# Combining three attention groups: pairs of token tiles share their small steps, and ScalarE makes the third product

## The reference, cut to what matters

```python
wts = jax.nn.softmax(jnp.stack(lses), axis=0)
attn = jnp.einsum('gbsh,gbshd->bshd', wts, jnp.stack(outs)).reshape(b, s, ATTN_WIDTH).astype(x.dtype)
attn_branch = jnp.einsum('bse,ed->bsd', attn * jax.nn.silu(gate_a), w_br_a)
```

## Time and profile before

| | |
|---|---|
| median of 3 runs | 2629.17 us |
| profiled execution, its own time | 2635.06 us |
| its span | 2633.3 us |
| TensorE matmul busy | 2522.2 us, 96% |
| VectorE busy | 1616.7 us, 61% |
| ScalarE busy | 938.1 us, 36% |
| GpSimd busy | 478.6 us, 18% |
| mean granted TensorE clock | 0.984 |

### The profile page before, as it was taken

The page is one execution under the profiler, slowest core; times in us unless marked ns, Lnnn a source line. Parts: engine busy times, 40 slices in busy tenths (PEclk is TensorE's granted clock), DMA queues, the critical chain, the costliest instruction groups (busy, mean ns, idle before and its releaser), DMA issues. The chain is left out here.

```text
span 2633.3 us, 36120 instructions
## 1 busy us (share of the span) xinstructions
PE 2522.2 (96%) x14232; PEld 1541.7 (59%) x14232; DVE 1616.7 (61%) x2315; ACT 938.1 (36%) x1823; POOL 478.6 (18%) x462
## 2 busy tenths in 40 slices
PE   7999998999999999999799999999879999999997
PEld 4444343356666767676688888655434444444586
DVE  5747656636565656565679999767873235533543
ACT  5322222235555555555643433322531113211232
POOL 0105554400000000010035354332100000000000
PEclk9999999999999999999899999999889999999999
DMA  5824545423333424243753434445431120110132
GB/s 195 303 96 157 204 152 176 180 96 109 127 131 117 145 102 169 104 166 120 255 207 117 176 129 146 159 160 188 157 106 60 34 80 29 36 33 32 57 97 80
DMA packets 145263, 341.26 MB, mean 130 GB/s; under 512 B 8137, under 2 KB 102581, under 8 KB 138056
## 3 DMA queue, kind: packets, MB, share of 16 engines
q1 hardware_dynamic: 126312, 238.94, 26.6%
q0 software_dynamic: 18640, 93.72, 9.3%
q10 hardware_dynamic: 144, 6.29, 0.7%
HBM read 215.10 MB, written 130.12 MB: 131 GB/s over the span
## 5 line engine op out<-in xcount | busy, mean ns | idle before, releaser
L1288 PE MATMUL ps<-mem 128*128 128x512 f16 (+1 forms) x9312 | 1750.2, 348 | 24.0 <-ACT mem L1671 5.8
L1288 PEld LDWEIGHTS ps<-mem 128*128 128x128 f16 x9312 | 928.1, 102 | 815.4 <-issue 83.2
L847 ACT ACTIVATE mem<-mem 128x2048 f16<-128x2048 f32 (+1 forms) x56 | 108.6, 1940 | 390.3 <-DVE mem L865 390.2
L2155 DVE TENSOR_TENSOR mem<-ps,mem 128x512 f32<-128x512 f32 (+2 forms) x144 | 79.8, 554 | 235.1 <-PE ps L1421 234.4
L872 DVE SCALAR_TENSOR_TENSOR mem<-mem 128x2048 f16<-128x2048 f32 (+1 forms) x56 | 132.7, 2369 | 80.1 <-ACT mem L847 80.1
L1772 ACT ACTIVATE mem<-ps 128x512 f32<-128x512 f32 (+1 forms) x144 | 72.1, 500 | 307.6 <-PE ps L1434 307.2
L835 POOL PARTITION_ALL_REDUCE mem<-mem x56 | 45.1, 807 | 750.9 <-DVE mem L828 725.1
L1540 PE MATMUL ps<-mem 128*128 128x256 f32 x768 | 171.4, 380 | 0.6
L1475 PE MATMUL ps<-mem 128*128 128x256 f32 (+1 forms) x640 | 168.7, 422 | 0.0
L1540 PEld LDWEIGHTS ps<-mem 128*128 128x128 f32 x768 | 144.5, 190 | 24.2 <-issue 5.5
L2190 DVE TENSOR_TENSOR mem<-mem 128x1024 f16<-128x1024 f32 x96 | 117.1, 1220 | 48.3 <-ACT mem L1793 47.8
(11 more groups left out here) (190 smaller groups left out, 2604.0 us busy)
## 6 DMA issues: line engine op xcount, KB each, us to landing
s_ks<-mem SPq DMA_DIRECT2D x96, 512.0 KB, 2.7
mem<-s_ks SPq DMA_DIRECT2D x23, 2048.0 KB, 9.0
mem<-in_w_in SPq DMA_DIRECT2D x44, 1024.0 KB, 6.3
s_sums<-mem POOLq DMA_DIRECT2D x24, 1024.0 KB, 4.3
mem<-s_sums SPq DMA_DIRECT2D x48, 512.0 KB, 3.9
s_uc<-mem POOLq DMA_DIRECT2D x24, 768.5 KB, 6.1
mem<-s_uc SPq DMA_DIRECT2D x18, 1024.0 KB, 7.3
s_og<-mem POOLq DMA_DIRECT2D x72, 132.0 KB, 2.6
```

Source lines behind the costliest of these rows:

```text
L847: act.activation(w_place(b)[:, 0, 0:chunks(b)], raw_of(b), ACT.Copy, scale=wscale[b % 3]).then_inc(S["w_hi"], 1)
L1288: mm = pe.matmul(out, lhs(a, k), rhs(b, k), start=(k == 0 and x == 0), stop=(k == kc - 1 and x == 2))
L2155: dve.tensor_tensor(l[:, :, c0:c1], ps[:, 2 + N % 2, :].rearrange("p (x c) -> p x c", x=2)[:, :, c0:c1], bias, ALU.add).then_inc(S["a_bias ...
```

## The change

- The tiles are taken in pairs. The minima, differences and weights of tiles t and t + 1 are computed together at the even tile, with 12 instructions on VectorE (before, 8 for each tile) and one exponential on ScalarE for both. The differences and the last products, which have one instruction before, have three, one for each group, with no wait between them.
- The wait for the loaded data is then for both tiles of the pair.
- The third group's product leaves VectorE. A new function `weigh(t)` on ScalarE makes it by eight Copy instructions of 128x64, each scaled by one head's weight, into `third[t % 2]`. VectorE waits for it (`g_third`) before its last sum.
- `weigh(0)` stands on ScalarE right behind `combine(0)` and `weigh(1)` before the sixth gate tile's evacuation; `weigh(x + 2)` stands where the list has `T` x. `combine` stands only where x is even.
- The buffers `ogt` and `cmb` have four tiles in place of two. GpSimd loads tiles 0 to 3 before the last store of `s_hy`, and tile t when tile t - 4 is combined. The places of `w_allmax` and `b_allmax` behind tiles 4, 6, 7 and 10 stay.

```diff
             def load_og(t):
-                pool.dma_start(ogt[t % 2], og_d[:, P * t:P * t + P, :, :].rearrange("g p a c -> p g a c")).then_inc(ld_og[t % 2], 16)
+                pool.dma_start(ogt[:, t % 4], og_d[:, P * t:P * t + P, :, :].rearrange("g p a c -> p g a c")).then_inc(ld_og[t // 2 % 2], 16)
...
-                        load_og(0)
-                        load_og(1)
+                        for t in range(4):
+                            load_og(t)
...
-            for t in range(2, NT):
-                pool.wait_ge(S["g_cmb"], t - 1)
+            for t in range(4, NT):
+                pool.wait_ge(S["g_cmb"], t - 3)
                 load_og(t)
                 if t in (4, 7):
                     w_allmax(pool, M0 + 3 + (t - 4) // 3)
...
-            def combine(t):
-                act.wait_ge(S["g_sc"], 2 * t + 1)
-                act.activation(wts[t % 2][:, 8:32], wts[t % 2][:, 8:32], ACT.Exp).then_inc(S["g_exp"], 1)
+            def combine(k):
+                act.wait_ge(S["g_sc"], 2 * k + 1)
+                act.activation(wts[k % 2][:, 16:64], wts[k % 2][:, 16:64], ACT.Exp).then_inc(S["g_exp"], 1)
+
+            def weigh(t):
+                act.wait_ge(S["g_sc"], 2 * (t // 2) + 2)
+                if t >= 2:
+                    act.wait_ge(S["g_cmb"], t - 1)
+                e = wts[t // 2 % 2][:, 16 + 24 * (t % 2) + 16:16 + 24 * (t % 2) + 24]
+                for j in range(2 * HH):
+                    op = act.activation(third[t % 2][:, HD * j:HD * j + HD], ogt[:, t % 4, 2, j // HH, HD * (j % HH):HD * (j % HH) + HD], ACT.Copy,
+                                        scale=e[:, j:j + 1])
+                op.then_inc(S["g_third"], 1)
...
-                if n in (3, 5):
-                    combine(n // 2 - 1)
+                if n == 3:
+                    combine(0)
+                    weigh(0)
+                if n == 5:
+                    weigh(1)
...
+                    if x % 2 == 0 and x + 2 < NT:
+                        combine(x // 2 + 1)
                     if x + 2 < NT:
-                        combine(x + 2)
+                        weigh(x + 2)
...
+                if t % 2 == 0:
...
+                    dve.wait_ge(ld_og[t // 2 % 2], 32 * (t // 4 + 1))
...
+                    for g in range(3):
+                        op = dve.tensor_tensor(both[:, :, g], low, nm[:, :, g], ALU.subtract)
...
+                    for g in range(3):
+                        op = dve.tensor_tensor(both[:, :, g], both[:, :, g], total, ALU.mult)
...
-                if t >= 2:
-                    m_wait(dve, POS["T", t - 2, 0])
+                if t >= 4:
+                    m_wait(dve, POS["T", t - 4, 0])
...
                 chain(dve.tensor_tensor(acc, acc, tmp, ALU.add))
                 settle()
-                weighted(tmp, 2)
-                settle()
-                dve.tensor_tensor(acc, acc, tmp, ALU.add).then_inc(S["g_cmb"], 1)
+                dve.wait_ge(S["g_third"], t + 1)
+                dve.tensor_tensor(acc, acc, third[t % 2], ALU.add).then_inc(S["g_cmb"], 1)
```

More of the change, by code:

```diff
@@ L431, in build @@
         gated = hg_tile(KD * len(SPANS) - 1)
[L432 to L435, removed]
+        ogt = mem[:, MERGED:MERGED + 4 * 6 * OW].rearrange("p (t g a c) -> p t g a c", t=4, g=3, a=2)
+        GSC = MERGED + 4 * 6 * OW
+        wts = [mem[:, GSC + 128 * i:GSC + 128 * i + 128] for i in range(2)]
+        cmb = [mem[:, GSC + 256 + 2 * AW * i:GSC + 256 + 2 * AW * (i + 1)].rearrange("p (a c) -> p a c", a=2) for i in range(4)]
+        third = [mem[:, GSC + 256 + 8 * AW + AW * i:GSC + 256 + 8 * AW + AW * (i + 1)] for i in range(2)]
+        assert GSC + 256 + 10 * AW <= OUT
         m16 = halves(mem[:, BASE:BASE + KD * T], KD, T)
@@ L453, in build @@
             p_first p_hi p_lo f_r f_im f_y f_post
-            ld_hx ld_ftab ld_itab g_cmb g_sc g_exp m_mul b_maxed b_alled b_scaled b_hi b_lo h_hi h_lo m_acc o_sq o_root o_r o_y""".split()
+            ld_hx ld_ftab ld_itab g_cmb g_third g_sc g_exp m_mul b_maxed b_alled b_scaled b_hi b_lo h_hi h_lo m_acc o_sq o_root o_r o_y""".split()
         S = {n: sem(n) for n in names}
@@ L1607, in _ @@
                 for j in range(4):
-                    mm = pe.transpose(ps[:, n % 8, P * j:P * j + P], cmb[x % 2][:, 0, P * j:P * j + P], ident)
+                    mm = pe.transpose(ps[:, n % 8, P * j:P * j + P], cmb[x % 4][:, 0, P * j:P * j + P], ident)
                 mm.then_inc(bank_ready[n % 8], 1)
@@ L2429, in _ @@
             for t in range(NT):
[L2430 to L2437, removed]
@@ L2438, in _ @@
-                settle()
[L2439 to L2452, removed]
-                if t >= 2:
-                    m_wait(dve, POS["T", t - 2, 0])
+                o, w = ogt[:, t % 4], wts[t // 2 % 2]
+                acc, tmp = cmb[t % 4][:, 0, :], cmb[t % 4][:, 1, :]
+                both = w[:, 16:64].rearrange("p (t g a h) -> p t g a h", t=2, g=3, a=2)
@@ new lines, in _ @@
+                e = both[:, t % 2]
+                if t % 2 == 0:
+                    two = ogt[:, t % 4:t % 4 + 2]
+                    nm, den = two[:, :, :, :, HW:HW + HH], two[:, :, :, :, HW + HH:OW]
+                    low, total = (w[:, c:c + 16].rearrange("p (t a h) -> p t a h", t=2, a=2) for c in (0, 112))
+                    ed = w[:, 64:112].rearrange("p (t g a h) -> p t g a h", t=2, g=3, a=2)
+                    dve.wait_ge(ld_og[t // 2 % 2], 32 * (t // 4 + 1))
+                    chain(dve.tensor_tensor(low, nm[:, :, 0], nm[:, :, 1], ALU.min))
+                    settle()
+                    chain(dve.tensor_tensor(low, low, nm[:, :, 2], ALU.min))
+                    settle()
+                    for g in range(3):
+                        op = dve.tensor_tensor(both[:, :, g], low, nm[:, :, g], ALU.subtract)
+                        if g < 2:
+                            chain(op)
+                    op.then_inc(S["g_sc"], 1)
+                    dve.wait_ge(S["g_exp"], t // 2 + 1)
+                    chain(dve.tensor_tensor(ed.rearrange("p t g a h -> p (t g) a h"), both.rearrange("p t g a h -> p (t g) a h"),
+                                            den.rearrange("p t g a h -> p (t g) a h"), ALU.mult))
+                    settle()
+                    chain(dve.tensor_tensor(total, ed[:, :, 0], ed[:, :, 1], ALU.add))
+                    settle()
+                    chain(dve.tensor_tensor(total, total, ed[:, :, 2], ALU.add))
+                    settle()
+                    chain(dve.reciprocal(total, total))
+                    settle()
+                    for g in range(3):
+                        op = dve.tensor_tensor(both[:, :, g], both[:, :, g], total, ALU.mult)
+                        if g < 2:
+                            chain(op)
+                    op.then_inc(S["g_sc"], 1)
+                    settle()
+                    dve.wait_ge(S["g_sc"], t + 2)
```

## The result

The changed kernel takes 2627.09 us, the median of 20 runs (2614.98 to 2631.49). The kernel before, run beside it, takes 2639.03 us in 20 runs (2629.15 to 2646.84). The ratio is 0.9949, 95% interval 0.9937 to 0.996, so the change makes it 0.5% faster: of 2639 us some 13.5 (10.6 to 16.6). The two medians differ by 11.9. The forecast was 11.4 less. The forecast time of 2617.8 us, with its range of 2612.5 to 2623.0, was missed, because it was built on the three runs of before that were shown (2629.17), and these are the three fastest of the 20.

A forecast was written before the change was run, and what follows sets the result against it. VectorE was taken to bound the combining stage's end; its terms summed to -11.25 us, a tile-by-tile walk gave 11.6 less, and -11.4 was taken from 2629.17 us: 2617.8 us, range 2612.5 to 2623.

The forecast's parts named there:

- start of tile 2: VectorE starts tile 2 at 1860.5 us instead of 1861.27, -0.8 us.
- five even rounds: VectorE's even rounds: small steps +0.54, third product -0.73, wait for copies +0.11; -0.08 us each, -0.4 in all.
- five odd rounds: VectorE's odd rounds lose small steps (1.94 us) and the third product (0.73); -2.67 us each, -13.35 in all.
- load 5 at the pair (4, 5): Load 5, queued on GpSimd behind `w_allmax`, lands late for the pair; +3.8 us, bounds 1.9 and 4.4.
- tile 10: VectorE's wait for the exponential at tile 10 begins 0.2 us later through longer steps; -0.2 us.
- wait for T 11: The last gate product's wait for TensorE's transposes, 0.67 us before, gets shorter; -0.3 us.
- ScalarE's copies: Third product on ScalarE: 346 ns a copy, eight in 2.1 us, 2.2 with handshakes; even tiles wait 0.1 us.
- the prediction's w: ScalarE-bound rival, chance 0.07: eight copies take w us, even tiles stall w - 2.0; even at 3.4, 9.8 us slower at 4.5.
- Tile 1: VectorE waits some 2 us for `third`, but the next gate product can't start before transposes and evacuation end anyway.
- The wait for load 11: Load 11 stands behind `b_allmax(1)`, but VectorE waits for ScalarE's `span_hi(1)` and exponential until about its landing.
- The tail: What follows the last gate product, up to TensorE's long run from 1969 us, is untouched, so its gain passes through.
- The drain behind a table load: Rival: each ScalarE table switch also empties the engine for another 1.28 us; gain only 2.9 us, 2626.3 us, chance 0.03.

The follow-up runs named there:

- the loads first: Changed kernel with GpSimd's maxima behind the loads of tiles 5, 7, 9, 11 instead of 4, 6, 7, 10; ratio to before 0.9927.
- the low half later: The loads first, tile 10's exponential before ScalarE's high half, third weight block's low half and next maximum behind tile 3, `weigh(3)` earlier; ratio to before 0.9922.
- eight copies' worth of 3 and 4 us: Changed kernel with four or eight extra unread ScalarE copies ahead of each tile's eight; stretches 116.25 and 123.02 us, ratios to before 0.9975 and 0.9995.

## Why the prediction was right, and where it was wrong

**The step that failed** is the last of the sum: "the median of the runs is 5.9 us lower, and I take the difference over unchanged: 2629.17 - 11.4 = 2617.8 us". The 11.4 us was near, the 2629.17 was not this kernel's usual time. Of 20 runs of before three are those I had; the median of all is 9.9 us above them, and the range was drawn round the three as if they were exact. They lie within 0.7 us of each other, where the 20 spread over 17.7. The first three runs of the changed kernel also lie within 0.7 us (2628.35 to 2629.01), so that by these threes alone the change would be worth 0.6 us. Three runs that agree don't show how far a kernel spreads. 2629.17 x 0.9949 would be 2615.8, inside the range. The profiled execution's own 2635.06 us, 5.9 off the three, was the hint that the kernel varies by more than three runs show, and I treated it as an offset of the profile. The change was mis-sized too, by less: 11.4 us against the stretch's 13.4, most of it a table load in the tail that the sum put at nothing (below).

The variation lies ahead of the stage. Over the twelve profiled executions the mark in front of tile 0 comes between 1837.1 and 1858.0 us, while what follows the stretch takes 662.7 to 665.6. Two places carry most of it. TensorE's last product of L1372 (L1374 after) starts at 497.3 us before, 498.6 in the changed kernel's first profile, 507.2 with the loads first and 491.3 with the low half later. In the changed kernel's first profile another 6.5 us of its 7.9 arise between there and the first matmuls of L1558, 1321.0 before and 1328.8 after; in the other eleven profiles this part takes 820.9 to 825.6 us, in that one 830.2. Two waits of ScalarE for stores to `s_ks` are longer there, and then the same 18 matmuls take TensorE almost twice as long, before and then after:

```profile
1293.14 1.06 ACT L1793 ACTIVATE mem<-mem 128x1024 f16<-128x1024 f32 x1 [3.66 <-DMA s_ks<-mem]
...
1304.34 1.06 ACT L1793 ACTIVATE mem<-mem 128x1024 f16<-128x1024 f32 x1 [1.16 <-DMA s_ks<-mem]
...
1307.16 2.13 PE L1288 MATMUL ps<-mem 128*128 128x256 f16 x18
```

```profile
1295.23 1.06 ACT L1795 ACTIVATE mem<-mem 128x1024 f16<-128x1024 f32 x1 [4.42 <-DMA s_ks<-mem]
...
1308.18 1.06 ACT L1795 ACTIVATE mem<-mem 128x1024 f16<-128x1024 f32 x1 [3.09 <-DMA s_ks<-mem]
...
1311.56 4.05 PE L1290 MATMUL ps<-mem 128*128 128x256 f16 x18
```

The clock granted over these 18 matmuls is 1.00 before and 0.50 after; TensorE had idled 0.84 us shortly before them in the one and 2.77 us in the other. The instructions there are the same in both kernels. Why the stores landed later in one execution than in the other stays open; no experiment was made on it.

**Point by point**, predicted and measured, from the mark to the last gate product:

| term | predicted | measured |
|---|---|---|
| start of tile 2 | -0.8 | -0.62 |
| five even rounds | -0.4 | -1.02 |
| five odd rounds | -13.35 | -13.44 |
| load 5 at the pair (4, 5) | +3.8 | +3.06 |
| tile 10 | -0.2 | -0.18 |
| wait for T 11 | -0.3 | -0.26 |
| ScalarE's high half at tile 5 | 0 | +0.36 |
| sum | -11.25 | -12.10 |
| the sigmoid's table load in the tail | 0 | -1.28 |
| whole stretch | -11.25 | -13.38 |

- *What bounds the stage.* Right: adding and taking work on VectorE moved the end in each experiment until TensorE's transposes came up.
- *ScalarE's copies.* Right in kind, 0.1 us too dear: 333 ns each in place of 346, eight in 2.02 us. This is just under VectorE's 2.05 us of two products and a sum, so no even tile waits. With eight copies' worth of 3 and 4 us (the prediction's w) even tiles wait 1.0 and 1.95 us, about the w - 2.0 of the prediction, and the stretch gets 6.5 and 13.3 us longer, so the cover ends at once behind 2.05 us. That the walk came out even at w = 3.4 was 0.6 us too early: at 4.0 it is even.
- *Tile 1.* Right: VectorE waits 1.85 us for `third`, but the gate product behind it waits for ScalarE's evacuation anyway (0.53 us).
- *The loads.* Right in cause and place, by the experiment; load 5 landed 5.5 us after its issue and not 6.6. The wait for load 11 (1.88 us) was foreseen as covered by ScalarE's high half, and was.
- *The tail.* Wrong: "untouched" it is on VectorE, but the change ends ScalarE's loop with a Sigmoid, where it ended with an Exp, and so takes a table load out of the chain that follows. That is 1.3 us that no term had.
- *The sum of the parts.* The prediction gave the moved product 0.73 us in each of ten rounds, 7.3 us. On top of the pairs this holds (7.0 us); alone the product is worth 2.9 us. The prediction names the reason, that half of the switches to Exp go with the pairs, but puts no number on it.
- *The rule on multiplications* from the Trainium skill (ScalarE: Activation LUTs, Rules for kernel authors), that they belong on VectorE: by price it holds here too, 2.02 us against 0.73. For the end of the stage it does not, since ScalarE had the time.
- *The drain behind a table load* from the Trainium skill (ScalarE: Activation LUTs, What ACT_TABLE_LOAD costs): this trace has none. The evacuation starts at 1874.29 us, 0.02 us behind the load of 1872.99 that took 1.28.

## What to carry to other kernels

Work may go to an engine that does it at three times the price, if it fits under what the bounding engine does before it asks for the result; measure that room, since behind it the cost comes back in full. When a consumer takes two tiles at once, a waiting queue entry between the two tiles' loads can become a wait of the pair: so it was behind loads 4 and 10, and not behind load 6, whose pair comes after a longer step. And a few microseconds on 2600 are to be read from a stretch between two marks of the trace; before giving a time in absolute terms, ask how far the runs of the old kernel spread.

## What the runs showed of the hardware

- Copies of 128x64 on ScalarE with a scale column that differs in each take 333 ns alone and follow each other each 0.24 us: (2.02 - 0.333) / 7.
- A load of 792 KB from `s_og` lands 4.9 us after its issue alone. Four issued one behind the other, beside a weight load and a store, land after 11.5 us for the last. The first pair waited 2.38 us for its loads in the changed kernel's first profile and 1.1 to 1.7 in others.
- Three all-reduces on GpSimd show 0.70 us in the changed kernel where before has 0.34. The profile calls GpSimd's spans rough, and nothing hung on it.
- Eighteen matmuls of 128x256 in fp16 take 2.13 us at a granted clock of 1.00 and 4.05 us at 0.50.
- Executions reach the stage up to 21 us apart, though the kernels are the same up to GpSimd's loads just ahead of it.
